# The last half instead of the last quarter of the MLP input by seven block products of eight, with the block sums placed anew

## The chip, the cores and the metric

One Trainium2 chip, one core. The metric is the time of one execution of the program on the device, in microseconds (us). The kernel before took 745.73 us (median of three runs, 745.73 to 746.08).

## The reference

A decoder layer on 512 tokens of width 1024, in float32. Only its frame matters here:

```python
h = rms_norm(x, pre_norm_mix)
y = hybrid_mixer(h, w_in, ..., w_branch_att, w_branch_dn, w_out)   # attention and DeltaNet, merged, @ w_out
x = x + rms_norm(y, post_norm_mix)
h = rms_norm(x, pre_norm_mlp)
y = jnp.square(jax.nn.relu(h @ w_mlp_in)) @ w_mlp_out               # 1024 -> 4096 -> 1024
x = x + rms_norm(y, post_norm_mlp)
```

## The kernel before, in words

**Products.** Every float32 operand is split into a high and a low part, and a product is made of three matmuls: high x high, high x low, low x high (`three`, L867 to L871, so every matmul of the MLP input shows as L869, L870 or L871).

**Units.** The weights stream through the core in units of 128 x 512 numbers (256 KB). For each unit SP issues a load into a raw buffer (`load`, L710; L785 and the lines behind it in the MLP input), ACT makes the high part (`copy`, L1372), POOL or DVE the low part by a subtraction (POOL L2480; DVE L1843 in the product with w_out), and PE multiplies. There are four buffers for raw and four for high and low parts: the load of unit u waits for the low part of unit u-4, the high part of u for PE to be done with unit u-4. Units 0 to 87 are w_in (`U_IN` = 88), 88 to 103 the two branch weights, 104 to 119 w_out (`U_BR` = 104; its first half, 104 to 111, is itself made by seven products of eight, from sums `o_sum`), and from 120 (`U_OUT`) on the MLP input. DVE and ACT make attention and DeltaNet beside the first two. Behind the loads of units 99 to 103 SP also issues four loads of residual rows (L770), one of the norm's weights (L772) and extra blocks of w_out (L716). Around the start of w_out ACT's order is written out: high of 106, two `o_hi`, high of 107, two `wo_hi`, high of 108; DVE makes the low parts of 108 to 110 then.

**MLP input.** Its 4096 columns are worked off in `G_PLAIN` = 12 plain groups of 256 columns (four units, 48 matmuls of 512 tokens each), and then in `STEPS_IN` = 2 steps (`PER_STEP` = 14 units each). A step makes 2 x 256 columns by a seven-product scheme: the 2 x 2 block product of a half of the rows and a half of the tokens is made with seven block products instead of eight (`q1` to `q7`, `IN_PRODUCTS`), over 256 tokens each, 168 matmuls a step. Four of the seven need a sum of two blocks of the token side (`t_full`, split by ACT into `ts_hi` and by DVE, L2264, into `ts_lo`; `t_low`) and four a sum of blocks of the weights (`u_sum`). Of a step's 14 low parts DVE makes ten (`in_low`) and POOL four. From the second group of units on eight raw buffers turn in a ring (`raw_of`, `raw_signal`, `RING` = 8).

**Block sums of weights.** They are made by DMA in DRAM beside the rest: SP copies one block (`u_copy`, L742, and `t_copy`, L739), POOL adds the other with an accumulating DMA (`u_add`, L2489; `add_sum`, L2476). `u_sum` serves the steps of the MLP input, the four sums v1, t3, t2, t4 (`t_sum` in the code: q = 0 to 3, in four quarters i = 0 to 3, 1 MB each) the MLP output, which is made by seven products of eight throughout. Where each copy and add is issued stands in tables by unit: `T_COPY_AT`, `IN_COPY_AT` for SP (behind that unit's load), `T_ADD_AT`, `IN_ADD_AT` for POOL (behind that unit's low part), `SUM_IN` for POOL by plain group. In all, SP's loads and copies go through the queue q1, and POOL's adds through q0.

## Time and profile before

| | us |
|---|---|
| median of the runs | 745.73 (745.73 to 746.08) |
| the profiled execution | 745.89 |
| its span | 744.2 |
| PE busy | 736.9 (99%) |
| weight loads of PE busy | 612.1 (82%) |
| DVE, ACT, POOL busy | 479.6, 401.2, 323.3 |

Matmuls overlap in the records: one of 512 columns is listed with 0.39 us, but they start 0.227 us apart. So a stretch of PE is measured from start to start. In a timeline a row has its start, its duration, the engine, the line and the operation; in brackets stands the idle time before it and what ended it. A row of DMA issues gives the size and the time from issue to landing.

### The profile page before, as it was taken

What the parts mean: (1) busy time and instruction counts of PE and PEld (TensorE: products, weight loads), DVE (VectorE), ACT (ScalarE), POOL (GpSimd) and SP (SyncE); (2) the same over time, 40 slices, a digit from 0 to 9 for tenths busy, and PEclk for the clock granted to TensorE, in tenths of its full rate; (3) what the DMA queues carried; (4) which work ended last, traced back from release to release, by engine and by line L of the source; (5) the groups of instructions that cost most, each with busy time, mean ns of one, the idle gap of its engine ahead of it and who ended that gap; (6) DMA issues with size and microseconds to landing.
All of it is one profiled execution on the core that took longest, in us unless ns stands there. A gap on an engine that the chain in (4) does not pass through costs nothing.

```text
span 744.2 us, 12157 instructions
## 1 busy us (share of the span) xinstructions
PE 736.9 (99%) x4312; PEld 612.1 (82%) x4312; DVE 479.6 (64%) x703; ACT 401.2 (54%) x653; POOL 323.3 (43%) x297
## 2 busy tenths in 40 slices
PE   9999999999999999999999999999999999999996
PEld 7788778888887878788888988888899988888885
DVE  5896899990454545454983612782257977778785
ACT  6657842268554455535664743343345665565671
POOL 2357894435454854564536574686422000000002
PEclk9999999999999999999999999999999999999999
DMA  9337458696566976785653689659556567774652
GB/s 339 106 93 251 155 174 310 217 264 162 119 189 180 265 202 158 217 240 186 221 184 85 184 222 272 156 142 225 142 156 201 181 211 235 245 248 148 218 177 113
DMA packets 57955, 145.00 MB, mean 195 GB/s; under 512 B 6545, under 2 KB 6961, under 8 KB 55601
## 3 DMA queue, kind: packets, MB, share of 16 engines
q1 hardware_dynamic: 52368, 118.39, 47.8%
q0 software_dynamic: 5200, 25.69, 17.3%
q8 instruction: 28, 0.46, 0.2%
q10 hardware_dynamic: 336, 0.28, 0.1%
q14 instruction: 23, 0.18, 0.1%
HBM read 140.12 MB, written 50.35 MB: 256 GB/s over the span
## 4 chain that ended last, share of the span: by engine, by line
PE 93%; POOL 3%; ACT 2%; DVE 1%; DMA 0%; issue 0%; SPq 0%; POOLq 0%; ACTq 0%; DVEq 0%
PE bank L869 28%; PE bank L870 27%; PE bank L871 27%; POOL rsq L2468 2%; PE bank L1116 1%; PE bank L1139 1%; PE bank L1126 1%; POOL w_lo L2480 1%; PE bank L1080 1%; PE bank L890 1%; PE bank L1044 1%; PE bank L896 1%; PE bank L1091 1%; PE bank L899 0%; PE bank L1178 0%; DMA raw<-in_w_in 0%
## 5 line engine op out<-in xcount | busy, mean ns | idle before, releaser
L2480 POOL TENSOR_TENSOR w_lo<-raw,w_hi 128x512 fp32r<-128x512 f32 x133 | 177.8, 1344 | 189.7 <-ACT w_hi L1372 187.9
L869 PE MATMUL bank<-h_hi,w_hi 128*128 128x512 f32 (+1 forms) x512 | 197.3, 385 | 0.2
L1372 ACT ACTIVATE w_hi<-raw 128x512 fp32r<-128x512 f32 (+2 forms) x190 | 129.9, 691 | 119.7 <-PE bank L871 106.6
L870 PE MATMUL bank<-h_lo,w_hi 128*128 128x512 f32 (+1 forms) x512 | 192.9, 377 | 0.0
L871 PE MATMUL bank<-h_hi,w_lo 128*128 128x512 f32 (+1 forms) x512 | 192.8, 376 | 0.0
L869 PEld LDWEIGHTS bank<-h_hi,w_hi 128*128 128x128 f32 x512 | 96.3, 188 | 23.5 <-issue 4.7
L871 PEld LDWEIGHTS bank<-h_hi,w_lo 128*128 128x128 f32 x512 | 96.3, 188 | 18.2
L870 PEld LDWEIGHTS bank<-h_lo,w_hi 128*128 128x128 f32 x512 | 96.5, 188 | 16.1
L1834 DVE SCALAR_TENSOR_TENSOR relu_sb<-bank,rs_ext 128x512 f32<-128x512 f32 (+1 forms) x28 | 17.0, 647 | 69.6 <-PE bank L871 57.5
L869 PE MATMUL bank<-w_hi,a_hi 128*128 128x512 f32 x120 | 46.8, 390 | 0.0
L871 PE MATMUL bank<-w_hi,a_lo 128*128 128x512 f32 x120 | 46.7, 389 | 0.0
L870 PE MATMUL bank<-w_lo,a_hi 128*128 128x512 f32 x120 | 46.7, 389 | 0.0
L2225 DVE TENSOR_TENSOR w_lo<-raw,w_hi 128x1024 fp32r<-128x1024 f32 (+1 forms) x32 | 36.8, 1156 | 7.6 <-ACT w_hi L1372 7.1
L1372 ACT ACTIVATE w_hi<-raw_m 128x512 fp32r<-128x512 f32 x36 | 22.6, 628 | 30.4 <-PE bank L871 30.0
L2480 POOL TENSOR_TENSOR w_lo<-raw_m,w_hi 128x512 fp32r<-128x512 f32 x20 | 31.5, 1581 | 16.8 <-ACT w_hi L1372 16.8
L869 PE MATMUL bank<-w_hi,h_hi 128*128 128x512 f32 x96 | 37.8, 393 | 0.0
L871 PE MATMUL bank<-w_hi,h_lo 128*128 128x512 f32 x96 | 37.4, 389 | 0.0
L870 PE MATMUL bank<-w_lo,h_hi 128*128 128x512 f32 x96 | 37.4, 389 | 0.0
L869 PE MATMUL bank<-wb_hi,a_hi 128*128 128x512 f32 x96 | 37.3, 389 | 0.0
L870 PE MATMUL bank<-wb_lo,a_hi 128*128 128x512 f32 x96 | 37.3, 389 | 0.0
L871 PE MATMUL bank<-wb_hi,a_lo 128*128 128x512 f32 x96 | 37.3, 389 | 0.0
L2632 POOL TENSOR_SCALAR ssh<-ssy 128x1 f32<-128x1 f32 x4 | 1.4, 343 | 77.8 <-ACT junk L1805 77.8
(360 smaller groups left out, 1471.1 us busy)
## 6 DMA issues: line engine op xcount, KB each, us to landing
raw<-in_w_in SPq DMA_DIRECT2D x87, 256.0 KB, 3.5
raw<-in_w_mlp_in SPq DMA_DIRECT2D x34, 256.0 KB, 2.9
raw<-in_w_mlp_out SPq DMA_DIRECT2D x26, 256.0 KB, 2.7
raw<-t_sum SPq DMA_DIRECT2D x26, 256.0 KB, 2.9
raw_m<-in_w_mlp_in SPq DMA_DIRECT2D x24, 256.0 KB, 3.8
v_sum<-in_w_mlp_out POOLq DMA_DIRECT2D x4, 1024.0 KB, 10.3
t_sum<-in_w_mlp_out POOLq DMA_DIRECT2D x4, 1024.0 KB, 10.4
t_sum<-v_sum POOLq DMA_DIRECT2D x4, 1024.0 KB, 10.8
```

The lines of the kernel that those rows point to most:

```text
L869: pe.matmul(o, s_hi, m_hi, start=start, stop=False, skip_group_check=True)
L870: pe.matmul(o, s_hi, m_lo, start=False, stop=False, skip_group_check=True)
L871: return pe.matmul(o, s_lo, m_hi, start=False, stop=stop, skip_group_check=True)
L890: pe.matmul(bank[banks[m]][:], w_hi[:, u, c[m]], h_hi[:, k, :], start=k == 0, stop=False, skip_group_check=True)
L896: pe.matmul(bank[banks[m]][:], w_lo[:, u, c[m]], h_hi[:, k, :], start=False, stop=False, skip_group_check=True)
L1044: x_ = pe.matmul(b[to, u % 16 * B32:u % 16 * B32 + B32], lhs, rhs, start=True, stop=True)
L1080: x_ = pe.matmul(b[:, pair * P:(pair + 1) * P], qk_dn[:, 4 * (1 - q) + pair, tok], state[:, pair, :], start=True, stop=True)
L1372: return a.activation(o, i_, ACT.Copy, scale=scale)
L1834: return v.scalar_tensor_tensor(out=o, in0=i0, scalar=s, in1=i1, op0=op0, op1=op1)
L2225: v.tensor_tensor(l, raw_part(s, n), h.bitcast(F32), ALU.subtract).then_inc(part_lo, n)
L2468: return g.tensor_tensor(dst, src, nhalf[:, 0:width], ALU.pow)
L2480: g.tensor_tensor(w_lo[:, u % 4, :], raw_of(u), w_hi[:, u % 4, :].bitcast(F32), ALU.subtract).then_inc(lo_ready, 1)
```

## The change

The plain groups are 8 instead of 12, the steps 4 instead of 2. The copies and adds for `u_sum` double (eight and eight, in two chunks each), and stand at units 13 to 32 and 50 to 80. The copies and adds for the MLP output's sums move: (q, i) = (1, 0) and (1, 1) are now added behind the low parts of units 97 and 101, (1, 2) behind the residual's part of w_out, (3, 1) to (3, 3) in the steps; the copies of (3, 2) and (3, 3) go behind the loads of units 112 and 116. The ring of eight raw buffers begins one group later. The blocks of the token side are split one by one in the last two plain groups.

```diff
--- before.py
+++ after.py
@@ -77,13 +77,14 @@
 U_DN = U_IN + 8
 U_BR = U_IN + 16
 U_OUT = U_BR + 16
-G_PLAIN = 12
+G_PLAIN = 8
 F_HALF = (FF - G_PLAIN * 256) // 2
 U_S = U_OUT + 4 * G_PLAIN
 STEPS_IN = F_HALF // 256
 PER_STEP = 14
 RING = 8
 CHUNKS = F_HALF // 512
+U_RING = U_OUT + 12
 U_M1 = U_S + STEPS_IN * PER_STEP
 NI = 8
 S_TWO = 64
@@ -92,16 +93,16 @@
 N_SUM = 4
 OUT_SUM_AT = {55: 0, 61: 1, 70: 2, 85: 3}
 OUT_ADD_AT = {u + 2: q for u, q in OUT_SUM_AT.items()}
-T_COPY_AT = {36: (0, 0), 38: (1, 0), 41: (0, 1), 43: (1, 1), 46: (0, 2), 48: (1, 2), 51: (0, 3), 53: (1, 3),
-             66: (2, 0), 72: (2, 1), 75: (2, 2), 78: (2, 3), 82: (3, 0), 88: (3, 1), 91: (3, 2), 94: (3, 3)}
-IN_COPY_AT = {27: 0, 29: 1, 31: 2, 34: 3}
-
-
-T_ADD_AT = {66: (0, 0), 75: (1, 0), 78: (0, 1), 81: (1, 1), 84: (0, 2), 90: (1, 2), U_OUT: (1, 3)}
-IN_ADD_AT = {50: 0, 53: 1, 60: 2, 70: 3}
-
-
-SUM_IN = {1: (2, 0), 2: (2, 1), 3: (2, 2), 4: (2, 3), 6: (3, 0), 7: (3, 1), 8: (3, 2), 9: (3, 3)}
+T_COPY_AT = {34: (0, 0), 36: (1, 0), 38: (0, 1), 41: (1, 1), 43: (0, 2), 46: (1, 2), 48: (0, 3), 51: (1, 3),
+             66: (2, 0), 73: (2, 1), 79: (2, 2), 86: (2, 3), 92: (3, 0), 96: (3, 1), 112: (3, 2), 116: (3, 3)}
+IN_COPY_AT = {13: (0, 0), 15: (0, 1), 17: (1, 0), 19: (1, 1), 21: (2, 0), 28: (2, 1), 30: (3, 0), 32: (3, 1)}
+
+
+T_ADD_AT = {74: (0, 0), 82: (0, 1), 90: (0, 2), 93: (0, 3), 97: (1, 0), 101: (1, 1), U_OUT: (1, 3)}
+IN_ADD_AT = {50: (0, 0), 53: (0, 1), 60: (1, 0), 65: (1, 1), 67: (2, 0), 69: (2, 1), 76: (3, 0), 80: (3, 1)}
+
+
+SUM_IN = {1: (2, 0), 2: (2, 1), 3: (2, 2), 4: (2, 3), 6: (3, 0)}
 X2_OUT = (4, 5)
 
 
@@ -612,19 +613,19 @@
 
     def raw_of(u):
 
-        r = (u - U_OUT) % RING
-        if u < U_OUT + RING or r >= RAW:
+        r = (u - U_RING) % RING
+        if u < U_RING or r >= RAW:
             return raw[:, u % RAW, :]
         return raw_m[r][:]
 
     def raw_signal(u):
 
-        r, turn = (u - U_OUT) % RING, (u - U_OUT) // RING
-        if u < U_OUT + RING:
+        r, turn = (u - U_RING) % RING, (u - U_RING) // RING
+        if u < U_RING:
             return raw_in[u % RAW], 16 * loads(u)
         if r >= RAW:
-            return raw_in[u % RAW], 16 * (loads(U_OUT + r) + turn)
-        return rawm_in[r], 16 + 16 * turn
+            return raw_in[u % RAW], 16 * (loads(U_RING - RING + r) + turn + 1)
+        return rawm_in[r], 32 + 16 * turn
 
     def low_of(u):
 
@@ -731,15 +732,17 @@
             if u == U_BR:
                 for q in range(2):
                     sp_.wait_ge(o_added[q], 32)
-                for q in (1, 2, 3):
-                    sp_.wait_ge(*added(q, 3 if q == 1 else 0))
+                for q in (2, 3):
+                    sp_.wait_ge(*added(q, 0))
+            if u == U_IN - 4:
+                sp_.wait_ge(*added(1, 0))
             load(u, u % RAW, unit_source(u), u - RAW + 1 if u >= RAW else None)
             if u in T_COPY_AT:
                 q, i = T_COPY_AT[u]
                 sp_.dma_start(*t_copy(q, i)).then_inc(t_copied[q], 16)
             if u in IN_COPY_AT:
-                q = IN_COPY_AT[u]
-                sp_.dma_start(*u_copy(q, 0)).then_inc(t_copied[2 + q % 2], 16)
+                q, chunk = IN_COPY_AT[u]
+                sp_.dma_start(*u_copy(q, chunk)).then_inc(t_copied[2 + q % 2], 16)
             if u in OUT_SUM_AT:
                 q = OUT_SUM_AT[u]
                 if q > 1:
@@ -780,8 +783,8 @@
         for g in range(2, G_PLAIN):
             for j in range(4):
                 u = U_OUT + 4 * g + j
-                if g > 2:
-                    sp_.wait_ge(*low_of(u - RING))
+                if g != 3:
+                    sp_.wait_ge(*low_of(u - RING if u > U_RING else u - RAW))
                 sp_.dma_start(raw_of(u), mlp_source(g, j)).then_inc(raw_signal(u)[0], 16)
                 if g in X2_OUT and j % 2:
                     t = 2 * X2_OUT.index(g) + j // 2
@@ -830,7 +833,7 @@
         sp_.wait_ge(unit_done, U_M1 - PER_STEP + 4)
         for s in (4, 5, 6, 7, 0, 1, 2, 3):
             if s < 4:
-                sp_.wait_ge(*low_of(U_M1 - RING + s + (U_S - U_M1 + RAW) % RING))
+                sp_.wait_ge(*low_of(U_M1 - RING + s))
             part(s, one_source(0, s))
         with sp_.Fori(1, NI) as i:
             one(i)
@@ -1639,7 +1642,7 @@
                 a.activation(act_pair(i * 2 + q, slice(4, 6) if m else slice(0, 3, 2)),
                              relu_sb[:, 2 * q + m, :].rearrange("p (s c) -> p s c", s=2), ACT.Square).then_inc(act_ready, 1)
 
-        def mlp_in(i, first, blocks=False):
+        def mlp_in(i, first):
             for j in range(8):
                 u = U_OUT + LEAD + j
                 if first and j == 7:
@@ -1654,12 +1657,14 @@
                     copy(w_hi[:, u % 4, :], raw_of(ahead)).then_inc(hi_ready, 1)
                 if j == 3 and not first or j == 7:
                     square_group(i, j // 4)
-                if blocks and j in (2, 3, 4, 5):
-                    a.wait_ge(diffs_made, OUT_G + j - 1)
-                    if j == 2:
-                        a.wait_ge(copied_out, 16 * (1 + NT))
-                    b = T_ORDER[j - 2]
-                    copy(ts_hi[b][:], t_full[b][:]).then_inc(dhi_ready, 1)
+
+        def block_high(n_):
+
+            a.wait_ge(diffs_made, OUT_G + n_ + 1)
+            if n_ == 0:
+                a.wait_ge(copied_out, 16 * (1 + NT))
+            b = T_ORDER[n_]
+            copy(ts_hi[b][:], t_full[b][:]).then_inc(dhi_ready, 1)
 
         def split_in(u):
 
@@ -1674,6 +1679,8 @@
                 split_in(u)
                 if j in (3, 7):
                     square_group(i, j // 4)
+                if j in (2, 3, 4, 5):
+                    block_high(j - 2)
 
         def square_in(s, e):
 
@@ -1714,10 +1721,7 @@
         mlp_in(0, True)
         with a.Fori(1, 3) as i:
             mlp_in(i, False)
-        mlp_in(3, False, True)
-        for i in range(4, G_PLAIN // 2 - 1):
-            mlp_in(i, False)
-        mlp_in_last(G_PLAIN // 2 - 1)
+        mlp_in_last(3)
         for s in range(STEPS_IN):
             mlp_in_step(s)
 
@@ -2338,16 +2342,10 @@
         combine(4)
         for i in range(4):
             t_low(i)
+        for u in range(U_S, U_S + LEAD):
+            in_low(u)
         relu(3, ms=(2, 3))
         combine(5)
-        for i in range(4, G_PLAIN // 2):
-            relu(i, ms=(0, 1))
-            combine(2 * i - 2)
-            if i == G_PLAIN // 2 - 1:
-                for u in range(U_S, U_S + LEAD):
-                    in_low(u)
-            relu(i, ms=(2, 3))
-            combine(2 * i - 1)
         for s in range(STEPS_IN):
             step_in(s)
         w_low(2, 1, 3)
@@ -2482,11 +2480,11 @@
             if u in T_ADD_AT:
                 add_sum(*T_ADD_AT[u])
             if u in IN_ADD_AT:
-                q = IN_ADD_AT[u]
-                g.wait_ge(t_copied[2 + q % 2], 32)
+                q, chunk = IN_ADD_AT[u]
+                g.wait_ge(t_copied[2 + q % 2], 32 * CHUNKS)
                 if q > 1:
-                    g.wait_ge(t_added[(2, 1)[q - 2]], 16)
-                g.dma_start(*u_add(q, 0), accum_op=ALU.add, max_dma_last_dim=8192).then_inc(t_added[(2, 3, 1, 2)[q]], 16)
+                    g.wait_ge(t_added[(2, 1)[q - 2]], 16 * CHUNKS)
+                g.dma_start(*u_add(q, chunk), accum_op=ALU.add, max_dma_last_dim=8192).then_inc(t_added[(2, 3, 1, 2)[q]], 16)
             if u in OUT_ADD_AT:
                 q = OUT_ADD_AT[u]
                 g.wait_ge(o_copied[q % 2], 16 * (q // 2 + 1))
@@ -2579,7 +2577,7 @@
         g.wait_ge(mlo_ready, 4)
         for e in range(2, 6):
             out_low(e)
-        add_sum(0, 3)
+        add_sum(1, 2)
         g.wait_ge(lo_ready, U_PLAIN + 4)
         for u in range(U_PLAIN + 4, U_OUT):
             split_u(u)
@@ -2621,6 +2619,8 @@
                     g.wait_ge(hi_ready, nth(u))
                     g.tensor_tensor(w_lo[:, u % 4, :], raw_of(u), w_hi[:, u % 4, :].bitcast(F32),
                                     ALU.subtract).then_inc(lo_ready, 1)
+                if s < 3 and v == 1:
+                    add_sum(3, s + 1)
         for t in range(NT):
             g.wait_ge(part_done, 24 + 8 * t)
             g.dma_start(x_res[:, t, :], x2_copy[t]).then_inc(late_in, 16)
```

## Rows read from the trace of the kernel before

**Rows 1.** The page, part 1: busy time and instructions of each engine.

```profile
PE 736.9 (99%) x4312; PEld 612.1 (82%) x4312; DVE 479.6 (64%) x703; ACT 401.2 (54%) x653; POOL 323.3 (43%) x297
```

**Rows 2.** Windows, groups 8 to 11 and steps: PE, PEld, DVE, ACT, POOL; clock, DMA.

```profile
501.73:545.25 43.52, 43.52 (x193) 36.04 (x192) 10.93 (x22) 14.60 (x24) 21.10 (x18) 1.00 0.71 175
545.25:585.56 40.31, 40.31 (x337) 40.31 (x336) 32.14 (x63) 22.45 (x39) 9.22 (x7) 1.00 0.55 170
```

**Rows 3.** Timeline of PE: first instruction of group 8, group 10, step 0, MLP output.

```profile
501.73 0.39 PE L869 MATMUL bank<-h_hi,w_hi 128*128 128x512 f32 x1
...
523.49 0.39 PE L869 MATMUL bank<-h_hi,w_hi 128*128 128x512 f32 x1
...
545.25 0.28 PE L869 MATMUL bank<-h_hi,w_hi 128*128 128x256 f32 x1
...
585.56 0.40 PE L869 MATMUL bank<-w_hi,a_hi 128*128 128x512 f32 x1
```

**Rows 4.** Timeline of DVE: the four lows of the block sums.

```profile
493.32 6.81 DVE L2264 TENSOR_TENSOR ts_lo<-t_full,ts_hi 128x1024 fp32r<-128x1024 f32 x4
```

**Rows 5.** DMA issues: a copy at 109 us, and the loads behind it.

```profile
v_sum<-in_w_mlp_out SPq DMA_DIRECT2D x1, 5.7
...
raw<-in_w_in SPq DMA_DIRECT2D x2, 256.0 KB, 5.2
```

**Rows 6.** SP's issue of unit 106's load (timeline), and its landing (DMA issues).

```profile
357.50 2.93 SPq L710 DMA_DIRECT2D raw<-t_out_sum  x2
...
raw<-t_out_sum SPq DMA_DIRECT2D x1, 256.0 KB, 3.4
```

**Rows 7.** Timeline of ACT from the high of unit 106 to that of 108.

```profile
366.20 0.63 ACT L1372 ACTIVATE w_hi<-raw 128x512 fp32r<-128x512 f32 x1 [1.14 <-PE bank L871]
366.74 1.57 ACT L1372 ACTIVATE o_hi<-m_mix 128x768 fp32r<-128x768 f32 x2
368.92 0.63 ACT L1372 ACTIVATE w_hi<-raw 128x512 fp32r<-128x512 f32 x1 [0.62 <-PE bank L871]
369.46 1.14 ACT L1372 ACTIVATE wo_hi<-wo_raw 128x512 fp32r<-128x512 f32 x2
370.50 0.62 ACT L1372 ACTIVATE w_hi<-raw 128x512 fp32r<-128x512 f32 x1
```

**Rows 8.** Timeline of POOL: lows of units 97 and 101.

```profile
342.43 1.29 POOL L2480 TENSOR_TENSOR w_lo<-raw,w_hi 128x512 fp32r<-128x512 f32 x1 [1.41 <-ACT w_hi L1372]
...
353.33 1.30 POOL L2480 TENSOR_TENSOR w_lo<-raw,w_hi 128x512 fp32r<-128x512 f32 x1 [1.42 <-ACT w_hi L1372]
```

**Rows 9.** DMA from 344 to 361 us: the queues (packets, MB, share of 16 engines).

```profile
q1 hardware_dynamic: 2016, 4.98, 81.0%
```

**Rows 10.** An add and a load at 410 us; then three loads (L710, 412.4 to 413.2).

```profile
t_sum<-in_w_mlp_out POOLq DMA_DIRECT2D x1, 1024.0 KB, 8.5
raw<-in_w_mlp_in SPq DMA_DIRECT2D x1, 256.0 KB, 2.7
...
DMA to landing us min/median/max: 6.6/6.9/8.3
```

**Rows 11.** Timeline of DVE: the lows of units 108 to 110.

```profile
372.20 3.01 DVE L1843 TENSOR_TENSOR w_lo<-raw,w_hi 128x512 fp32r<-128x512 f32 x3
```

**Rows 12.** Timeline of PE: first instructions of units 106 and 108.

```profile
371.38 0.39 PE L869 MATMUL bank<-w_hi,o_hi 128*128 128x512 f32 x1
...
374.10 0.46 PE L869 MATMUL bank<-w_hi,o_hi 128*128 128x512 f32 x1
```

**Rows 13.** Timelines of ACT and DVE: the high and the low of unit 113.

```profile
379.57 0.63 ACT L1372 ACTIVATE w_hi<-raw 128x512 fp32r<-128x512 f32 x1 [0.41 <-DMA raw<-in_w_out]
...
382.17 1.29 DVE L1843 TENSOR_TENSOR w_lo<-raw,w_hi 128x512 fp32r<-128x512 f32 x2
```

**Rows 14.** The page, part 6: landing of the first adds.

```profile
v_sum<-in_w_mlp_out POOLq DMA_DIRECT2D x4, 1024.0 KB, 10.3
```

## The prediction

> **What bounds the kernel now.** I read the page first: TensorE (PE) is busy for 736.9 of 744.2 us, and no other engine is above two thirds [rows 1]. So a time can only be won by giving PE less to do, and can only be lost by letting it wait. Next, the windows by stage: in the last two plain groups and in the two steps PE is busy for the whole stretch, at a granted clock of 1.00, the upper of its levels (2.4 GHz) [rows 2]. The plain groups have idle time on the weight loads (36.04 of 43.52 us); the steps have none (40.31 of 40.31). That is why a step is priced below by its row and not by its columns.
>
> The profiled execution took 745.89 us, for a span of 744.2 us; it stands 0.16 us above the median of the runs, 745.73. I make the sum against 745.89 and take the 0.16 off at the end.
>
> **The plain groups that go, the steps that come.** Groups 8 to 11 are replaced by steps of the same kind as the two that exist. The first PE instructions of group 8, of group 10, of step 0 and of the MLP output are in [rows 3]. Two groups, 10 and 11, take 545.25 − 523.49 = 21.76 us: 96 matmuls of 512 columns at 227 ns. The two steps take 585.56 − 545.25 = 40.31 us, 20.16 each: 168 matmuls of 256 columns at 120 ns. A step does the work of two groups, so each swap gives 1.61 us, and two give **−3.2 us**. (By columns alone, seven eighths of 21.76, it would be 2.72 each and 5.4 in all; the weight-load row says that the step doesn't get it.) The number of PE instructions should grow by 2 x (168 − 96) = 144, from 4312 to 4456.
>
> **Work beside PE in the steps.** DVE makes 10 of 14 lows and the block combinations of a step; in the two steps it was busy for 32.14 of 40.31 us [rows 2]. The two new steps have the same per-step work, with 8 us of room in 40, so I cost it at nothing. New is what stands ahead of step 0: the four lows of the block sums (t_low) now run beside group 7, and the lows of the first units of step 0 must follow them. The four ended at 493.32 + 6.81 = 500.13 [rows 4], and group 8 started at 501.73 [rows 3]; one low of 512 columns is 0.7 us, so the first is ready at 500.8, 0.9 us early. Below: 0; above: 1 us, if POOL's lows, slowed beside those wide DVE operations, slip. I take 0, as the row gives a margin. The three adds (3,1) to (3,3), one a step, come among loads that are issued eight units ahead, 8 x 20.16 / 14 = 11.5 us, and the worst landing beside an add was 8.3 [rows 10]: 0. On POOL each waits for sums ordered a plain group or more before, and behind it stand the step's lows: 0, and up to 1 us if a sum were late. The loads of group 2 now wait for the low four units back, 4 x 43.52 / 16 = 10.9 us of PE's time ahead, for a load of 2.7: 0.
>
> **DMA in the input product (units 0 to 93).** There are now eight copies and eight accumulating adds for the MLP input instead of four and four, and the copies for the MLP output move; of the adds for the MLP output four are left here instead of six. A copy of 1 MB landed in 5.7 us and the loads behind it in 5.2 instead of 2.7 [rows 5, 10]. A load there has more room than that: the load of unit 106 landed at 357.50 + 3.4 = 360.9 and its high part was made at 366.20 [rows 6, 7], 5.3 us of room and units of the input product are loaded by the same rule. One copy (2.5 us) or one add (below, some 5 us) fits in; two adds don't, unless the units are spread over a longer time, which between units 50 and 90 they are, as attention and DeltaNet work lies between them. Cost: nothing, covered by this room; without it an add would cost up to what it lacks, 0 to 1 us each.
>
> **The adds at units 97 and 101.** Here I put the loss. Add (1,0) is issued by POOL behind the low of unit 97, which ended at 342.43 + 1.29 = 343.72; add (1,1) behind the low of unit 101, now at 353.33 + 1.30 = 354.63 [rows 8]. Before, no add stood in this stretch: the queue of SP alone held 81% of the 16 DMA engines from 344 to 361, with 4.98 MB of residual rows, branch weights and w_out [rows 9]. What an add does to loads is seen once: add (1,3), issued at 410 us, landed in 8.5 us, and a load issued beside it in 2.7; but the three loads issued 412.4 to 413.2 landed in 6.6 to 8.3 us, median 6.9 [rows 10]. So an add of 1 MB costs what is behind it from 3.9 (6.6 − 2.7) to 5.6 us (8.3 − 2.7). I take 5.0, towards the upper end, as the queue here is dense. The train has no gap to absorb it, so unit 106's load lands at 360.9 + 2 x 5.0 = 370.9; with 3.9 at 368.7, with 5.6 at 372.1.
>
> From there the engines' order decides. ACT makes the high part of 106 (0.63), then, in its written order, two o_hi (1.57), the high of 107 (0.63), two wo_hi (1.14), the high of 108 (0.62): 4.6 us [rows 7]. Then DVE makes the low of 108 (three in 3.01 us, the first somewhat longer beside POOL; I take 1.4) [rows 11]. So unit 108 is ready at 370.9 + 6.0 = 376.9, and PE wanted it at 374.10 [rows 12]: a stall of **2.8 us**; 0.6 with the low bound, 4.0 with the high one. Unit 106 itself is ready at 370.9 + 0.63 + 1.30 = 372.8 against 371.38 [rows 12], 1.4 us of the same 2.8. After the stall everything is late alike, and the next thing to be late would be the second half of w_out, units 113 on.
>
> The Trainium skill says another thing of the queues ("DMA: Bandwidth & Descriptors", section "Queues, rings and completion order"): each DMA engine goes round-robin between the queues that have work, packet by packet. By it a load on SP's queue would pass an add on POOL's with half of the engines' time; as an estimate from that rule it loses half, 2.5 us, to each add, and the sum would be 742.5. The three loads at 412 us disagree with it, the one at 410 does not.
>
> **The copy at unit 112.** Copy (3,2) now stands ahead of the loads of units 113 on; they land 2.5 us (5.2 − 2.7) to 3.0 (5.7 − 2.7) later. The high of 113 was made at 379.57 + 0.63 = 380.20, and DVE came to its low only at 382.17 [rows 13]: 2.0 us of room, so 0.5 to 1.0 us over, less what PE itself is behind. If the stall of 2.8 is there, this is covered; I take 0, range 0 to 1.0. SP's new wait at unit 84 is for the adds at units 67 and 69, fifteen units earlier, and what is queued behind it on SP is the load of unit 84 alone: 0. Of the three waits at unit 104 one goes, where PE had no stall: 0.
>
> **Sum:** 745.89 − 3.2 + 2.8 = 745.5, less 0.16: **745.3 us**. About 0.2% (1.5 us) is what a measurement of this kernel can tell from no change, so the sum is "no change".
>
> **The rivals.** (B) The loads get through beside the adds, and each add costs them less than 2.6 us: unit 106 lands before 360.9 + 5.3 = 366.2, when ACT comes to it, and there is no stall. Then only the copy at 112 is left, 0 to 1.0: 742.5 (745.7 − 3.2) to 743.5. For it: add and load at 410 landed side by side. Against it: the three loads behind. The skill's round-robin rule would give this rival. Chance 0.30.
> (C) Slower. The same place, but an add holds the queue longer than at 410, where it ran on an empty queue: the adds in the input product landed in 10.3 us and more by the page [rows 14], 1.8 more than 8.5. At 5.0 + 1.8 = 6.8 each, unit 106 lands at 374.5, the stall is 6.4, and the time 745.73 − 3.2 + 6.4 = 748.9. It comes out over the 1.5 us from a stall of 4.7, a landing at 372.8, 5.95 us per add. Range 747.2 to 749. Against it: the landing time holds waiting as well as moving. Chance 0.13.
> (D) The steps gain less than they should: a new step runs late for its block sums or its lows (0 to 1 us at step 0, or an add (3,1) to (3,3) among its loads), without the stall at 106 to 108: 743 to 745. Chance 0.03.
>
> **How the numbers follow.** A (the sum) 0.54, its own range 745.7 − 3.2 + 0.6 = 743.1 to 745.7 − 3.2 + 4.0 = 746.5. B 0.30, C 0.13, D 0.03. The likeliest is A, so 745.3. The range runs from B's low end, 742.4, to just over A's high one, 747.0, and leaves most of C out. Faster by over 0.2% (under 744.24): B, and that part of A and D with a stall under 1.7: 0.38. Slower by over 0.2% (above 747.22): 0.13. The rest 0.49.
>
> **What would show it.** Right: PE x4456; a step still at 20.16 us; PE idle for 2 to 4 us between 370 and 378 with w_lo from POOL or DVE as releaser; loads of units 104 to 107 landing in 6 to 12 us; POOL idle before the low of 106 released by DMA through ACT. Wrong: PE without a stall there, and loads issued beside the adds in 3 to 5 us (B); a stall at units 97 to 103 or at 113 to 116 instead; a gap at step 0; steps away from 20.16 us.

## The result and the profile after

The kernel after takes 750.64 us (median of 6 runs, 749.79 to 751.30), before 745.73; the ratio is 1.0061 (95% interval 1.0048 to 1.0074). So it is slower by 4.9 us, where no change (745.3) was forecast and 747.0 was the upper end of the range. The profiled execution took 749.80 us for a span of 748.1: it lies 3.9 us above the profiled one of before and at the low end of its own runs. The account below is of these 3.9; the remaining 1.0 us of the medians is in no profile (the slowest of the six runs shows a mean granted clock of 0.993, against 0.998 in the profiled one).

The page of the kernel after (busy time, DMA queues, and the chain's shares by engine):

```profile
PE 735.7 (98%) x4456; PEld 616.0 (82%) x4456; DVE 499.9 (67%) x743; ACT 408.6 (55%) x669; POOL 316.1 (42%) x293
...
q1 hardware_dynamic: 55184, 125.73, 48.9%
q0 software_dynamic: 6288, 29.89, 20.1%
...
PE 84%; DMA 5%; POOL 5%; ACT 2%; DVE 2%; issue 1%; SPq 0%; ACTq 0%; POOLq 0%; DVEq 0%
```

PE has less to do (735.7 against 736.9 us) and 144 instructions more, as forecast [rows 1]. But the chain that ended last now has 5% of DMA, which stood at 0% before, and PE only 84%, where it had 93%.

First the steps. The window from the first instruction of step 0 to that of the MLP output (columns as in [rows 2]):

```profile
508.75:589.45 80.70, 80.70 (x673) 80.68 (x672) 64.44 (x123) 44.98 (x79) 21.31 (x17) 1.00 0.73 220
```

Four steps take 80.70 us, 20.18 each, with the weight loads as busy as PE; before, the same work took 585.56 − 501.73 = 83.83 us [rows 3]. The gain is 3.1 us, as the sum had it. All that is lost is lost before the steps: they start at 508.75 instead of 501.73, 7.0 us late. What PE waited for in the kernel after (us in total, times, the longest):

```profile
PE bank L872 <- POOL w_lo L2478: 3.8, 3, 1.8
...
PE bank L872 <- ACT x_o L1375: 0.8, 1, 0.8
```

Beside these, instruction by instruction, PE is later than before by 0.3 us from its first units on (a difference from run to run), by 1.9 more from 349.15, by 3.2 more from 373.98 to the low parts of w_out's first units, and by 1.5 more from 386.14 and at unit 113: 6.9 in all. The third of these was forecast at 2.8 us, the last at 0; for the 1.9 at 349.15 the sum had no term.

**The stall at 349 us.** Timelines of ACT, DVE and PE of the kernel after:

```profile
344.52 0.63 ACT L1375 ACTIVATE w_hi<-raw 128x512 fp32r<-128x512 f32 x1 [4.55 <-DMA raw<-in_w_branch_dn]
345.06 1.04 ACT L1375 ACTIVATE y_hi<-qk_dn 128x1024 fp32r<-128x1024 f32 x1
...
346.20 1.40 DVE L2076 TENSOR_TENSOR y_lo<-qk_dn,y_hi 128x1024 fp32r<-128x1024 f32 x1 [5.07 <-ACT y_hi L1375]
347.64 2.87 DVE L2071 TENSOR_TENSOR gate_a<-bank,gate_a 128x512 f32<-128x512 f32 x4
...
349.15 0.47 PE L872 MATMUL bank<-y_hi,w_hi 128*128 128x512 f32 x1 [1.77 <-POOL w_lo L2478]
```

ACT waits 4.55 us for the load of unit 97 and makes its high part at 344.52. Behind it in ACT's order stands `y_hi` (345.06), DVE can make `y_lo` only at 346.20, and behind that in DVE's order stand the `gate_a` products that free a bank; by their mean length two of the four are done at 349.1, and PE goes on at 349.15. The row names POOL as the releaser, whose low ended 0.4 us earlier; the times fit DVE's second product, which is argued from the times alone. SP, too, waits for `y_lo` before the first residual row, so the whole train of loads sets out at 347.63, 2.8 us later than before. The DMA issues of the kernel after, from issue to landing (an add with the load issued beside it at 334.7, the add of unit 97 at 346.5, a load behind it at 348.0, the add of unit 101 with the load of 105 at 360.2, the load of 106 at 362.4):

```profile
v_sum<-in_w_mlp_out POOLq DMA_DIRECT2D x1, 1024.0 KB, 11.3
raw<-in_w_branch_dn SPq DMA_DIRECT2D x1, 256.0 KB, 9.7
...
t_sum<-in_w_mlp_out POOLq DMA_DIRECT2D x1, 1024.0 KB, 8.3
...
raw<-in_w_branch_dn SPq DMA_DIRECT2D x1, 256.0 KB, 8.1
...
t_sum<-in_w_mlp_out POOLq DMA_DIRECT2D x1, 1024.0 KB, 11.3
raw<-v_out_sum SPq DMA_DIRECT2D x1, 256.0 KB, 11.6
...
raw<-t_out_sum SPq DMA_DIRECT2D x1, 256.0 KB, 10.2
```

The load of unit 97, issued 0.1 us after add (0,3), lands 9.7 us later, at 344.5. In the kernel before, the same load (issued at 334.47) and ACT's high part of it were:

```profile
raw<-in_w_branch_dn SPq DMA_DIRECT2D x1, 256.0 KB, 3.3
...
341.72 0.63 ACT L1372 ACTIVATE w_hi<-raw 128x512 fp32r<-128x512 f32 x1 [2.07 <-PE bank L871]
```

It had landed at 337.8, so unit 97 had 3.9 us of room, and a landing 6.7 us later is 2.8 us too late. The load stood behind copy (3,1) in SP's queue. The trace has the copy as 16 packets of 65536 bytes, some 2.8 us each, and until 338.7 no packet of the add. From 340 to 344 both queues move (packets, MB, share of 16 engines):

```profile
q0 software_dynamic: 92, 0.75, 92.2%
q1 hardware_dynamic: 87, 0.16, 13.4%
```

The packets of the two are about as many, but one of the add has 8192 bytes and one of a load 2048. So the load lost its time twice: first behind the copy, and then taking turns with the add.

**The stalls from 374 us on.** PE and ACT of the kernel after:

```profile
373.98 0.50 PE L872 MATMUL bank<-w_hi,o_hi 128*128 128x512 f32 x1 [1.42 <-POOL w_lo L2478]
...
376.20 0.50 PE L872 MATMUL bank<-w_hi,o_hi 128*128 128x512 f32 x1 [0.57 <-POOL w_lo L2478]
...
384.49 0.64 ACT L1375 ACTIVATE w_hi<-raw 128x512 fp32r<-128x512 f32 x1 [2.67 <-DMA raw<-in_w_out]
385.02 1.06 ACT L1375 ACTIVATE x_o<-bank 128x512 f32<-128x512 f32 x2
...
386.14 0.50 PE L872 MATMUL bank<-wo_hi,o_hi 128*128 128x512 f32 x1 [0.81 <-ACT x_o L1375]
```

Unit 105's load lands at 360.31 + 11.6 = 371.9 and unit 106's at 362.38 + 10.2 = 372.6, where 370.9 was forecast for 106. Then ACT's written order follows as forecast, until PE has unit 108 5.2 us late. The wait at 386.14 is of another kind: ACT waits 2.67 us for the load of unit 112, and `x_o`, which PE needs, stands behind that unit's high part.

### The profile page after: what moved, and what is told of

Its sections match the earlier page's. It is cut to its first block, busy times and chain, and to the rows that moved or that the text cites. A ratio compares the mean times of both kernels' runs of the same rounds, so it can differ in the third digit from the quotient of the medians.

```text
span 748.1 us, 12517 instructions
## 1 busy us (share of the span) xinstructions
PE 735.7 (98%) x4456; PEld 616.0 (82%) x4456; DVE 499.9 (67%) x743; ACT 408.6 (55%) x669; POOL 316.1 (42%) x293
## 4 chain that ended last, share of the span: by engine, by line
PE 84%; DMA 5%; POOL 5%; ACT 2%; DVE 2%; issue 1%; SPq 0%; ACTq 0%; POOLq 0%; DVEq 0%
PE bank L872 25%; PE bank L874 24%; PE bank L873 24%; DMA raw<-in_w_branch_dn 2%; POOL w_lo L2478 2%; POOL rsq L2466 2%; DMA raw<-v_out_sum 2%; PE bank L1119 1%; PE bank L1142 1%; PE bank L1129 1%; PE bank L1083 1%; DMA raw<-in_w_out 1%; PE bank L893 1%; PE bank L1047 1%; PE bank L899 1%
## 5 line engine op out<-in xcount | busy, mean ns | idle before, releaser
L2478 POOL TENSOR_TENSOR w_lo<-raw,w_hi 128x512 fp32r<-128x512 f32 x125 | 168.0, 1354 | 177.0 <-ACT w_hi L1375 175.3
L1375 ACT ACTIVATE w_hi<-raw 128x512 fp32r<-128x512 f32 (+2 forms) x198 | 135.0, 689 | 130.4 <-PE bank L874 90.6
L872 PE MATMUL bank<-h_hi,w_hi 128*128 128x512 f32 (+1 forms) x496 | 186.0, 375 | 0.2
L873 PE MATMUL bank<-h_lo,w_hi 128*128 128x512 f32 (+1 forms) x496 | 181.6, 366 | 0.0
L874 PE MATMUL bank<-h_hi,w_lo 128*128 128x512 f32 (+1 forms) x496 | 181.5, 366 | 0.0
L872 PEld LDWEIGHTS bank<-h_hi,w_hi 128*128 128x128 f32 x496 | 93.5, 189 | 20.8 <-issue 4.7
L873 PEld LDWEIGHTS bank<-h_lo,w_hi 128*128 128x128 f32 x496 | 93.7, 189 | 13.8
L1838 DVE SCALAR_TENSOR_TENSOR relu_sb<-bank,rs_ext 128x512 f32<-128x512 f32 (+1 forms) x24 | 13.3, 594 | 41.5 <-PE bank L874 29.4
L872 PE MATMUL bank<-ts_hi,w_hi 128*128 128x256 f32 x128 | 36.3, 284 | 0.0
L873 PE MATMUL bank<-ts_lo,w_hi 128*128 128x256 f32 x128 | 36.2, 283 | 0.0
```

Of the source, the lines that this page charges most:

```text
L872: pe.matmul(o, s_hi, m_hi, start=start, stop=False, skip_group_check=True)
L873: pe.matmul(o, s_hi, m_lo, start=False, stop=False, skip_group_check=True)
L874: return pe.matmul(o, s_lo, m_hi, start=False, stop=stop, skip_group_check=True)
L1375: return a.activation(o, i_, ACT.Copy, scale=scale)
L1838: return v.scalar_tensor_tensor(out=o, in0=i0, scalar=s, in1=i1, op0=op0, op1=op1)
L2478: g.tensor_tensor(w_lo[:, u % 4, :], raw_of(u), w_hi[:, u % 4, :].bitcast(F32), ALU.subtract).then_inc(lo_ready, 1)
```

## The experiments

Theory Q is that an accumulating add keeps the DMA engines from the loads behind it. Rival K is that the copies do it, in the queue that they share with the loads; rival S, that the steps or the larger number of sums cost the time. The parts `T_ADD_AT`, `SUM_IN`, `T_COPY_AT` are those of the kernel after.

**1. The adds of units 97 and 101 moved.**

```diff
-T_ADD_AT = {74: (0, 0), 82: (0, 1), 90: (0, 2), 93: (0, 3), 97: (1, 0), 101: (1, 1), U_OUT: (1, 3)}
-SUM_IN = {1: (2, 0), 2: (2, 1), 3: (2, 2), 4: (2, 3), 6: (3, 0)}
+T_ADD_AT = {74: (0, 0), 82: (0, 1), 90: (0, 2), 93: (0, 3), U_OUT: (1, 3)}
+SUM_IN = {1: (2, 0), 2: (2, 1), 3: (2, 2), 4: (2, 3), 5: (1, 0), 6: (3, 0)}
-                if s < 3 and v == 1:
-                    add_sum(3, s + 1)
+                if v == 1:
+                    add_sum(*((3, s + 1) if s < 3 else (1, 1)))
```

> The kernel after, with the adds (1,0) and (1,1) moved from units 97 and 101 to plain group 5 and to step 3. Theory Q (an accumulating add keeps the DMA engines from the loads behind it, some 8 us each): the loads of units 100 to 106 land as before, PE's 3.1 us of waiting around units 105 to 109 go, and most of the 12.1 us that ACT waits for branch weights; what is left is the 1.9 us at unit 96, and the 1.5 us at units 112 and 113 stay or grow to 2: 745.5 to 747.5. Rival K (the copies behind units 96 and 112 do it, in SP's own queue): the adds don't matter, 749 to 751. Rival S (the steps or their sums cost the time): 749 to 751, with PE's waits unchanged.

Measured: 749.81 us (748.13 to 751.03), ratio 1.0049 (1.0034 to 1.0063). A miss, outside Q's 745.5 to 747.5. PE's wait and three of its matmuls in this run:

```profile
PE bank L872 <- POOL w_lo L2478: 3.6, 1, 3.6
...
350.79 0.47 PE L872 MATMUL bank<-y_hi,w_hi 128*128 128x512 f32 x1 [3.58 <-POOL w_lo L2478]
...
352.16 0.63 PE L874 MATMUL bank<-y_hi,w_lo 128*128 128x512 f32 x1
352.58 0.63 PE L872 MATMUL bank<-y_hi,w_hi 128*128 128x512 f32 x1
```

The number is the one that K and S gave; the waits are not. The stalls at 104 to 109 are gone, as Q said, and so is the one at 112 and 113, which Q had left standing; but PE comes to these units 5.5 us late, so neither shows what its cause is worth. The load of unit 97 landed later still, and PE stood for 3.6 us instead of 1.8, at the same place. From then on two starts lie 0.43 us apart instead of 0.23. The windows before, in and after that stretch:

```profile
346.80:351.00 4.20, 0.62 (x3) 0.24 (x2) 3.04 (x4) 4.07 (x8) 3.78 (x3) 1.00 0.18 55
352.00:353.00 1.00, 1.00 (x3) 0.73 (x3) 0.14 (x1) 0.00 (x0) 0.00 (x0) 0.50 1.08 336
356.00:358.00 2.00, 2.00 (x11) 1.62 (x10) 0.00 (x0) 1.25 (x3) 1.30 (x1) 1.00 1.01 385
```

The granted clock was 1.00 while PE idled, 0.50 (1.2 GHz) from 352 to 355, and 1.00 again from 356: the wait of 3.6 us cost a further 1.6 us. So this run says little of the price of the two adds, as another stall grew.

**2. The copies of units 112 and 116 moved** into plain groups 3 and 4, behind SP's load of (g, j) = (3, 2) and (4, 2).

```diff
-             66: (2, 0), 73: (2, 1), 79: (2, 2), 86: (2, 3), 92: (3, 0), 96: (3, 1), 112: (3, 2), 116: (3, 3)}
+             66: (2, 0), 73: (2, 1), 79: (2, 2), 86: (2, 3), 92: (3, 0), 96: (3, 1)}
                 sp_.dma_start(raw_of(u), mlp_source(g, j)).then_inc(raw_signal(u)[0], 16)
+                if (g, j) in {(3, 2): (3, 2), (4, 2): (3, 3)}:
+                    q, i = {(3, 2): (3, 2), (4, 2): (3, 3)}[g, j]
+                    sp_.dma_start(*t_copy(q, i)).then_inc(t_copied[q], 16)
```

> The kernel after, with the copies (3,2) and (3,3) moved from units 112 and 116 to plain groups 3 and 4. Theory Q: only the last stall goes, 1.1 us at unit 112 and 0.4 at unit 113: 748.3 to 749.5. Rival K (the copies are what is late): also the stall at 104 to 108 shrinks, under 748. If the stall at 112 is only the earlier one handed on, nothing changes: 750.6.

Measured: 749.23 us (748.73 to 750.87), ratio 1.0047 (1.0034 to 1.0061): by the medians 1.4 less than the kernel after, in Q's range, but the two intervals overlap. In the profiled run the wait of `x_o` at unit 112 stays (0.7 us); the one at 113 is gone, and PE loses 1.0 us there instead of 1.5. So by the traces a third of the last stall is the copies', and the rest is handed on by the train ahead.

**3. The copy of unit 96 moved** to plain group 3 in the same way; the add at 93 stays.

```diff
-             66: (2, 0), 73: (2, 1), 79: (2, 2), 86: (2, 3), 92: (3, 0), 96: (3, 1), 112: (3, 2), 116: (3, 3)}
+             66: (2, 0), 73: (2, 1), 79: (2, 2), 86: (2, 3), 92: (3, 0), 112: (3, 2), 116: (3, 3)}
```

> The kernel after, with the copy (3,1) moved from unit 96 to plain group 3; the add (0,3) at unit 93 stays. Theory Q: add (0,3) then starts on an empty queue and lands after some 8 to 9 us instead of 11.3, the load of unit 97 at 343 instead of 344.5; ACT, which waits for it with y_hi behind, is 1.5 us earlier; of the 1.9 us at unit 96 0 to 0.6 are left: 749 to 750. Rival K (the copy alone makes the wait): the load of unit 97 lands at 338 to 339 and the stall of 1.9 is gone and the train behind is earlier too, 747.5 to 748.8.

Measured: 746.69 us (745.06 to 747.49, 12 runs), ratio 1.0010 (1.0001 to 1.0018). One copy of 1 MB, 3.9 us of the 4.9. It went beyond both expectations. PE's waits, and the landing of unit 97's load:

```profile
PE bank L875 <- POOL w_lo L2481: 1.0, 2, 0.6
PE bank L875 <- DVE w_lo L1850: 0.6, 1, 0.6
...
raw<-in_w_branch_dn SPq DMA_DIRECT2D x1, 256.0 KB, 4.0
```

The load lands in 4.0 us although the add was issued just before it, and there is no wait at unit 96. The stalls left, 2.2 us at 106 to 109 and 1.2 at 112 and 113, stand where the forecast had its two terms.

**4. All of it moved out of units 93 to 119.**

```diff
-T_ADD_AT = {74: (0, 0), 82: (0, 1), 90: (0, 2), 93: (0, 3), 97: (1, 0), 101: (1, 1), U_OUT: (1, 3)}
-SUM_IN = {1: (2, 0), 2: (2, 1), 3: (2, 2), 4: (2, 3), 6: (3, 0)}
+T_ADD_AT = {74: (0, 0), 82: (0, 1), 90: (0, 2), U_OUT: (1, 3)}
+SUM_IN = {1: (1, 0), 2: (1, 1), 3: (1, 2), 4: (2, 0), 5: (2, 1), 6: (2, 2)}
+SUM_STEP = {(0, 1): (2, 3), (1, 1): (3, 0), (2, 1): (3, 1), (2, 8): (3, 2), (3, 1): (3, 3)}
-        add_sum(1, 2)
+        add_sum(0, 3)
-                if s < 3 and v == 1:
-                    add_sum(3, s + 1)
+                if (s, v) in SUM_STEP:
+                    add_sum(*SUM_STEP[s, v])
```

The copies (3,1), (3,2), (3,3) go behind the loads (3, 2), (5, 2) and (7, 2) of the plain groups.

> The kernel after, with all that stood in units 93 to 119 moved away: adds (0,3), (1,0), (1,1) and copies (3,1), (3,2), (3,3) go to the end of w_out, the plain groups and the steps. Theory Q: PE has none of the three stalls, and the gain of two steps is left, 3.0 to 3.2 us: 742.3 to 743.0. Rival S (steps with less gain, or adds in the steps late): PE waits at step 0 or in the steps, 744 to 746.

Measured: 742.53 us (741.83 to 743.13), ratio 0.9951 (0.9939 to 0.9963): faster than both kernels. Busy times and PE's one wait, which is that of the kernel's start:

```profile
PE 733.7 (99%) x4456; PEld 616.3 (83%) x4456; DVE 499.8 (67%) x743; ACT 408.9 (55%) x669; POOL 314.5 (42%) x293
...
PE bank L1155 <- DVE ones L1847: 1.1, 1, 1.1
```

The two further steps are worth 3.3 us once their sums stand elsewhere. Rival S, that the steps or the sums as such cost the time, falls.

**5. The kernel before with adds (1,0) and (1,1) at units 97 and 101**, still 12 plain groups and 2 steps.

```diff
-T_ADD_AT = {66: (0, 0), 75: (1, 0), 78: (0, 1), 81: (1, 1), 84: (0, 2), 90: (1, 2), U_OUT: (1, 3)}
+T_ADD_AT = {66: (0, 0), 78: (0, 1), 84: (0, 2), 90: (1, 2), 97: (1, 0), 101: (1, 1), U_OUT: (1, 3)}
-                for q in (1, 2, 3):
-                    sp_.wait_ge(*added(q, 3 if q == 1 else 0))
+                for q in (2, 3):
+                    sp_.wait_ge(*added(q, 0))
+            if u == U_IN - 4:
+                sp_.wait_ge(*added(1, 0))
```

> The kernel before (12 plain groups, 2 steps), with nothing changed but the adds (1,0) and (1,1), from units 75 and 81 to 97 and 101 (and the wait that goes with them from unit 104 to 84). Theory Q: loads behind the two adds wait some 8 us each, as in the run with the copy at 96 moved, and PE waits 2 to 2.4 us at units 106 to 109, once more up to 0.6 at unit 112 or 113: 747.5 to 748.8. Rival S (the lateness comes with the steps, their sums or the longer list of adds): 745.7 to 746.2, no wait of PE.

Measured: 748.86 us (747.83 to 749.54, 5 runs), ratio 1.0043 (1.0030 to 1.0056), 0.1 above the upper end of Q's range: the two adds alone make the old kernel 3.0 us slower.

**6. The adds of `add_sum` in rows of at most 2048**, and **10. of at most 1024**.

```diff
-            g.dma_start(*t_add(q, i), accum_op=ALU.add, max_dma_last_dim=8192).then_inc(t_added[q], 16)
+            g.dma_start(*t_add(q, i), accum_op=ALU.add, max_dma_last_dim=2048).then_inc(t_added[q], 16)
```

> The kernel after, with the adds of add_sum in rows of at most 2048 instead of 8192 (max_dma_last_dim), so in four times as many descriptors. If the engines take turns between the queues by descriptor, a load now gets through four times sooner beside an add: loads issued behind an add land in 4 to 7 us, and the stalls at unit 96 and 104 to 109 shrink: 745 to 748. If an add has all of an engine's work until it is done, whatever its pieces, loads still land after the add, and as smaller pieces cost more each, the add takes 9 to 14 us instead of 8: 751 to 756.

> The kernel after, with the adds of add_sum in rows of at most 1024 (8192 in the kernel after; 2048 gave 746.6 us). If smaller pieces go on letting loads through, the load of unit 97 lands before 341, the loads behind the add at unit 97 well before that add, and the time is 743 to 746; the add takes over 12 us. If the pieces' own cost takes over, the queue holds the engines longer in all and the train of loads at 345 to 361 is later: 748 to 755.

Measured: 746.61 us (744.05 to 749.14, 12 runs) with 2048, ratio 1.0008 (0.9997 to 1.0020), and 746.82 (745.74 to 748.38, 11 runs) with 1024, ratio 1.0015 (1.0006 to 1.0024): in the first range of run 6, and between the two of run 10. Some 4 us of the 4.9 come back with one number changed. In both traces the load of unit 97 lands in 6.9 us instead of 9.7, with no wait at unit 96, and that of unit 105 in 7.7 and 6.4 instead of 11.6. How the DMA queues share the engines while the add of unit 97 and the loads behind it both move (packets, MB, share of 16 engines), in the kernel after from 351 to 353 us:

```profile
q0 software_dynamic: 34, 0.28, 70.9%
q1 hardware_dynamic: 32, 0.13, 17.3%
```

with rows of 2048, from 349 to 353:

```profile
q0 software_dynamic: 226, 0.46, 62.2%
q1 hardware_dynamic: 230, 0.66, 45.9%
```

and with rows of 1024, from 349 to 353:

```profile
q1 hardware_dynamic: 306, 0.87, 60.8%
q0 software_dynamic: 311, 0.32, 50.4%
```

In each stretch the two queues moved about as many packets. A packet of the add is as long as its row (0.28 MB in 34 packets is 8.2 KB), one of the loads has 2048 or 4096 bytes. So the queues take turns by packets, and the length of the row sets the share of the loads: 0.07 MB a microsecond in the kernel after, 0.17 and 0.22 with the smaller rows. The add took longer (10.9 and 15.5 us instead of 8.3), and the loads issued from 344 to 353 landed no sooner than in the kernel after (7.4 to 14.0 us after their issue, against 7.8 to 12.0).

The turns don't explain the beginning. From 347 to 351 in the kernel after the queue of the loads has no packet:

```profile
q0 software_dynamic: 78, 0.64, 89.0%
```

The first load of the train was issued at 347.63, and its first packet moves at 351.5, 3.9 us later; in the kernel before, with no add, it took 0.9 us (344.84 to 345.8). What holds it back wasn't tried. 1024 gains nothing more: PE's clock fell in its profiled run behind a stall of 1.9 us, and the spread of these runs is wide.

**7. The add of unit 93 moved** to the end of w_out; the copy at 96 stays.

```diff
-T_ADD_AT = {74: (0, 0), 82: (0, 1), 90: (0, 2), 93: (0, 3), 97: (1, 0), 101: (1, 1), U_OUT: (1, 3)}
-SUM_IN = {1: (2, 0), 2: (2, 1), 3: (2, 2), 4: (2, 3), 6: (3, 0)}
+T_ADD_AT = {74: (0, 0), 82: (0, 1), 90: (0, 2), 97: (1, 0), 101: (1, 1), U_OUT: (1, 3)}
+SUM_IN = {1: (1, 2), 2: (2, 0), 3: (2, 1), 4: (2, 2), 5: (2, 3), 6: (3, 0)}
-        add_sum(1, 2)
+        add_sum(0, 3)
```

> The kernel after, with the add (0,3) moved from unit 93 to the end of w_out ((1,2) and (2,0) to (2,3) each a plain group later); the copy (3,1) stays behind unit 96. Theory Q (it takes the copy and the add together to make unit 97 late): the load of unit 97 lands at 339 to 341, no stall at unit 96; the stalls of 2.0 to 2.6 at 106 to 109 and 0.6 to 1.3 at 112 and 113 stay: 745.5 to 747.5. If the copy alone makes it late: 750, a stall at unit 96.

Measured: 747.02 us (744.79 to 748.19, 11 runs), ratio 1.0012 (1.0003 to 1.0020). PE's waits:

```profile
PE bank L872 <- POOL w_lo L2478: 1.8, 2, 1.3
...
PE bank L872 <- ACT x_o L1375: 1.0, 1, 1.0
```

No wait at unit 96. The time is in Q's range. Taking away the copy alone (run 3) gives 3.9 us and the add alone 3.6: it takes both.

**8. Only the copies of 112 and 116 left**, the copy of 96 and the adds of 97 and 101 moved as in runs 1 and 3; the add at unit 93 stays.

> The kernel after, with the adds (1,0) and (1,1) and the copy (3,1) moved out of units 93 to 103 (add (0,3) at unit 93 stays); what is left of the crowd is the copies (3,2) and (3,3) behind units 112 and 116. This gives the price of these copies alone, with PE on time before them. The forecast put it at 0 to 1.0: 742.5 to 743.6, with PE waiting at unit 112 or 113 if at all. If they cost what PE lost there in the kernel after, 1.3 to 1.5: 743.8 to 744.2.

Measured: 743.78 us (743.11 to 744.97, 8 runs), ratio 0.9972 (0.9962 to 0.9982). PE's wait:

```profile
PE bank L875 <- DVE w_lo L1850: 1.1, 1, 1.1
```

One stall of 1.1 us, at unit 113, just over the forecast's 0 to 1.0, and 1.2 us by the medians against run 4.

**9. The copy of unit 96 three units later.**

```diff
-             66: (2, 0), 73: (2, 1), 79: (2, 2), 86: (2, 3), 92: (3, 0), 96: (3, 1), 112: (3, 2), 116: (3, 3)}
+             66: (2, 0), 73: (2, 1), 79: (2, 2), 86: (2, 3), 92: (3, 0), 99: (3, 1), 112: (3, 2), 116: (3, 3)}
```

> The kernel after, with the copy (3,1) issued behind the load of unit 99 instead of unit 96, three units later, where SP is idle for some 6 us until the load of unit 100. Theory Q, refined (a copy that stands ahead of loads just as an add starts gets the add in front of those loads): no load stands between copy and add, unit 97's load lands before 340, no stall at unit 96. The copy has landed before the loads of 345 to 361: 746.5 to 747.7, as with the copy moved far away. If the copy in this crowd costs time wherever it stands: 749 to 751.

Measured: 748.31 us (747.60 to 748.97), ratio 1.0033 (1.0020 to 1.0045), between the two expectations. The copy's landing and PE's waits:

```profile
t_sum<-in_w_mlp_out SPq DMA_DIRECT2D x1, 10.6
...
PE bank L872 <- POOL w_lo L2478: 2.2, 1, 2.2
...
PE bank L872 <- DVE w_lo L1847: 1.1, 1, 1.1
```

The stall at unit 96 is gone, so the order of copy, load and add was its cause. But the copy landed at 349.3, not before the train: it had waited behind the add of 93, the add of unit 97 came behind it, and PE waited 2.2 us at unit 104, with the clock down behind it. The refined theory was right on the place and missed that the queue has no gap there either.

**11 and 12. The adds put back into version 4**, that of unit 97 alone, and both.

```diff
-T_ADD_AT = {74: (0, 0), 82: (0, 1), 90: (0, 2), U_OUT: (1, 3)}
-SUM_IN = {1: (1, 0), 2: (1, 1), 3: (1, 2), 4: (2, 0), 5: (2, 1), 6: (2, 2)}
+T_ADD_AT = {74: (0, 0), 82: (0, 1), 90: (0, 2), 97: (1, 0), U_OUT: (1, 3)}
+SUM_IN = {2: (1, 1), 3: (1, 2), 4: (2, 0), 5: (2, 1), 6: (2, 2)}
```

With both, `101: (1, 1)` stands in `T_ADD_AT` too, and `2: (1, 1)` goes out of `SUM_IN`.

> The version with everything moved out of units 93 to 119 (742.5 us), with the add (1,0) put back behind unit 97 and nothing else. The forecast's step: a load has 5.3 us of room and one add costs it some 5, so one add fits: loads of units 100 to 103 land 5 us later than without it, PE does not wait, 742.3 to 743.0. If one add is enough to make PE late, 743.3 to 744.5.

Measured: 742.52 us (742.24 to 743.68, 11 runs), ratio 0.9954 (0.9940 to 0.9969): the add is free. PE waits only at the kernel's start (1.1 and 0.5 us). The load of unit 100:

```profile
raw<-in_w_branch_dn SPq DMA_DIRECT2D x1, 256.0 KB, 8.5
```

> The same version with the adds (1,0) and (1,1) put back behind units 97 and 101, no add at 93 and no copy at 96, 112 or 116. It is the forecast's likeliest case by itself: a stall of 2.8 us (0.6 to 4.0) at units 106 to 109, 745.3. From the runs since, the stall is some 2.0 to 2.4: 744.4 to 745.3. If the two adds cost what they did in the kernel before (+3.0): 745.5.

Measured: 746.23 us (744.71 to 747.78, 12 runs), ratio 1.0000 (0.9985 to 1.0014), above all three figures expected, of which the highest was 745.5. The loads of units 104 and 105, the add between them, and PE's waits:

```profile
raw<-in_w_out SPq DMA_DIRECT2D x1, 256.0 KB, 11.5
...
t_sum<-in_w_mlp_out POOLq DMA_DIRECT2D x1, 1024.0 KB, 11.5
raw<-v_out_sum SPq DMA_DIRECT2D x1, 256.0 KB, 11.7
...
PE bank L876 <- POOL w_lo L2482: 1.4, 3, 0.6
...
PE bank L876 <- ACT x_o L1379: 0.2, 1, 0.2
```

The first add costs nothing and the second 3.7 us. Unit 104's load, issued 1.8 us ahead of the second add, lands in 11.5 us, unit 105's in 11.7 and unit 106's in 10.2, within the forecast's 6 to 12. In this trace PE loses 2.9 us at units 104 to 109 and 0.5 more from 382.5 on, where `x_o` stands behind unit 112's high part; the profiled run (745.75) lies 0.5 below the median.

## Why the prediction was wrong

**The gain was right.** −3.2 was forecast for two steps; the windows give 3.1, version 4 gives 3.3 by the medians. 4456 instructions, 20.2 us a step, no gap at step 0: right.

**The adds at 97 and 101: mechanism right, size near.** 2.8 us (0.6 to 4.0) was forecast at units 106 to 109. In the kernel with nothing else there (run 12) the price is 3.7, in the old kernel 3.0. That one add fits in and two don't holds: 0 and 3.7. By the medians the term was 0.9 too small; in the trace of run 12 the stall itself is 2.9, and what is missing is the 0.5 handed on to the second half of w_out, which was named and given no price. With this term alone the kernel would be at 746.2, inside the range.

**What failed is the step on "DMA in the input product (units 0 to 93)".** It stopped at unit 93 and cost its copies and adds at nothing, because one copy or one add fits into the room of a load, and said itself that two adds don't. Then the part on the adds began at unit 97. The copy (3,1) at unit 96, put beside add (0,3) of unit 93, is in neither. SP issued it 0.8 us ahead of that add, and the load of unit 97 right behind both; it landed 9.7 us after its issue instead of 3.3. The room was also taken from another unit: 5.3 us is that of unit 106, and unit 97 had 3.9. Two things made this dear. ACT holds `y_hi` behind that unit's high part, so that 2.8 us of lateness went through DVE to PE (1.9 us of stall) and to SP, which holds the residual rows for `y_lo`. And with the whole train 2.8 us later the stall behind it was 3.2 us, where it was 2.2 in run 3 and 3.0 in run 7. Removed alone, the copy gives back 3.9 us.

**The copy at 112, cost 0 as "covered", was so only in part.** By itself, with the one at 116, it costs 1.2 us (run 8; 0 to 1.0 was the bound). Beside the stall of 106 to 109 the copies cost 0.5 us by the traces of the kernel after and run 2 (1.4 by the medians, with overlapping intervals), and from run 12 to run 3, which has the copies and the add (0,3) more, 0.5 by the medians (746.23 to 746.69), less than the runs' spread. So the stall covers about half of their price; the room doesn't grow by as much as PE is late. A likely reason, not tested, is that SP's next loads wait for low parts and so are late too.

**The rivals.** Rival C (slower, 0.13) came true in sign; its range, 747.2 to 749, ended 1.6 us below the measured time, and its reason, a longer hold of each add, isn't what the traces show. The adds of units 93 and 101 did land in 11.3 us, that of 97 in 8.3 (8.5 alone), but the difference is waiting: the add issued at 360.23 moves its first packet at 364.6 and lands 6.9 us later, the one issued at 346.47 moves its first at 348.0 and lands 6.8 us later. The stall that C asked for at 106 to 108 was 6.4 us; there were 3.2, and the rest came from places that it didn't name.

For B, the page of the Trainium skill that was weighed ("DMA: Bandwidth & Descriptors", section "Queues, rings and completion order") has each engine go round-robin between its queues by packets. The traces agree in the counts: 34 packets to 32 in the kernel after, 226 to 230 in run 6, 311 to 306 in run 10 (that a packet of the trace is one of the page's isn't shown). What didn't hold is the estimate made from the rule, that a load keeps half of the engines' time: with packets of 8192 bytes against 2048 or 4096 it kept 17.3%, against 70.9% for the add, and its first packets came late besides. The three loads at 412 us, read as speaking against the rule, show the same two things: their first packet moved at 416.0, 3.6 us after the first of them was issued, and from 415.9 to 417 their queue moved 23 packets to 20 of the add.

**Open:** the load of unit 97 landed at 344.5 in the kernel after and at 346.2 in run 1, with the same copy and the same add before it, and the runs of each kernel with a crowd spread over 1.5 to 5 us. What decides it wasn't tried, nor whether the copy in smaller packets than 65536 bytes would let the load of unit 97 through.

## What to carry to other kernels

Count the room of each load in microseconds (here 3.9 at unit 97, 5.3 at unit 106) and lay against it every bulk transfer that is in flight in that span, copies on the load's own queue and adds on another alike: here one was free, and the second cost 3 to 4 us. Cut the table at no boundary of the code: look at each pair of neighbours, and at what stands behind the late tile in each engine's order. Where bulk transfers can't be moved, smaller rows give the small loads their turn.

## What the runs showed of the hardware

- While an accumulating DMA of 1 MB and loads of another queue both moved, the two had about as many packets (34 to 32, 226 to 230, 311 to 306 for rows of 8192, 2048 and 1024), so the share went by their length: the loads moved 0.13 MB in 2 us, and 0.66 and 0.87 MB in 4 us. The add took 8.3, 10.9 and 15.5 us.
- A transfer issued while another queue kept the engines busy moved its first packet 3.9 us after its issue (the loads at 347.63) and 4.4 (the add at 360.23), where a load on idle engines took 0.9 (before, 344.84).
- After a wait of 3.6 us TensorE ran at 0.50 of its clock for some 3.4 us (run 1), which cost 1.6 us more; behind the wait of 1.8 us in the kernel after it kept its clock of 1.00. Behind waits of 2.2 and 1.9 us (runs 9 and 10) it was 0.50 too, from 372.2 to 375.6 and from 377.3 to 380.7, and some 1.5 us more were lost.
